# Decoder trunk on one core: ScalarE makes the high part of h, and the last norm's products are split over two engines

## What is computed

```
def rmsnorm(x, g):
    y = xf * lax.rsqrt(jnp.mean(xf * xf, axis=-1, keepdims=True) + EPS)
    return (y * g)
def swiglu(h, w_gu, w_down):
    gate, up = jnp.split(h @ w_gu, 2, axis=-1)
    return (jax.nn.silu(gate) * up) @ w_down
def layer(...):
    x = x + 0.5 * swiglu(rmsnorm(x, n1), ffn1_gu, ffn1_down)
    h = rmsnorm(x, n_mix)            # then h @ w_in, gated linear attention, window attention
    x = x + concatenate([o_g, o_s]) @ w_out
    x = x + 0.5 * swiglu(rmsnorm(x, n2), ffn2_gu, ffn2_down)
# after both layers: y = rmsnorm(x, norm_final)
```

## Time and profile before

| | us |
|---|---|
| runs of the kernel | 2183.99, 2188.75, 2182.62 |
| median | 2183.99 |
| profiled execution, span from first to last instruction | 2178.1 |
| TensorE busy in the span | 2116.3 (97%) |
| VectorE, ScalarE, GpSimd busy | 811.9, 581.5, 800.7 |

### The profile page before, as it was taken

How to read it: one execution, slowest core, us unless ns; L and a number is a source line. 1 busy time by engine, 2 the same in 40 slices (tenths; PEclk the granted TensorE clock), 3 DMA queues, 4 the chain that set the end, 5 groups by cost and what they waited for, 6 DMA issues and landing times.

```text
span 2178.1 us, 40378 instructions
## 1 busy us (share of the span) xinstructions
PE 2116.3 (97%) x16718; PEld 2078.8 (95%) x16718; DVE 811.9 (37%) x1125; ACT 581.5 (27%) x795; POOL 800.7 (37%) x337
## 2 busy tenths in 40 slices
PE   6999999999999999999999999999999999999996
PEld 6999999998889999999999999999898999999996
DVE  5222222486257222222332222226754452222224
ACT  3222222235233222222232222222532322222222
POOL 3333344432113333344433333444221233444443
PEclk9999999999889999999999999999997999999998
DMA  4222222421212222222222222233221122222222
GB/s 137 90 87 87 87 87 97 132 78 50 81 51 78 87 88 88 88 93 97 89 87 87 87 88 88 96 96 123 69 90 39 61 88 87 87 87 87 92 92 99
DMA packets 56869, 190.53 MB, mean 87 GB/s; under 512 B 8976, under 2 KB 10672, under 8 KB 56240
## 3 DMA queue, kind: packets, MB, share of 16 engines
q1 hardware_dynamic: 48960, 176.31, 25.0%
q10 hardware_dynamic: 7824, 13.00, 1.8%
HBM read 184.37 MB, written 6.95 MB: 88 GB/s over the span
## 4 chain that ended last, share of the span: by engine, by line
PE 92%; DVE 6%; issue 1%; ACT 0%; DMA 0%; DVEq 0%; ACTq 0%
PE ps L379 84%; DVE h_hi L989 2%; PE ps L538 1%; DVE ssum L1003 1%; PE ps L651 1%; PE ps L527 1%; DVE h_lo L992 1%; PE ps L444 1%; PE ps L645 1%; PE ps L690 1%; PE ps L718 0%; PE ps L510 0%; DVE x L1323 0%; PE ps L679 0%; PE ps L704 0%
## 5 line engine op out<-in xcount | busy, mean ns | idle before, releaser
L366 POOL TENSOR_TENSOR w_lo<-w_raw,w_hi 128x1024 fp32r<-128x1024 f32 x332 | 800.3, 2411 | 1359.4 <-ACT w_hi L745 1345.2
L379 PE MATMUL ps<-h_hi,w_hi 128*128 128x272 f32 x3424 | 718.8, 291 | 23.8 <-DVE h_lo L992 22.1
L379 PE MATMUL ps<-h_lo,w_hi 128*128 128x272 f32 x3424 | 712.9, 290 | 0.0
L379 PE MATMUL ps<-h_hi,w_lo 128*128 128x272 f32 x3424 | 710.8, 289 | 0.0
L745 ACT ACTIVATE w_hi<-w_raw 128x1024 fp32r<-128x1024 f32 x328 | 347.5, 1060 | 1349.2 <-PE ps L379 1349.1
L379 PEld LDWEIGHTS ps<-h_hi,w_hi 128*128 128x128 f32 x3424 | 544.1, 190 | 28.8 <-issue 24.8
L379 PEld LDWEIGHTS ps<-h_hi,w_lo 128*128 128x128 f32 x3424 | 543.4, 190 | 0.0
L379 PEld LDWEIGHTS ps<-h_lo,w_hi 128*128 128x128 f32 x3424 | 538.9, 190 | 0.0
L379 PE MATMUL ps<-act_lo,w_hi 128*128 128x272 f32 x1408 | 291.6, 289 | 0.0
L379 PE MATMUL ps<-act_hi,w_hi 128*128 128x272 f32 x1408 | 291.2, 288 | 0.0
L379 PE MATMUL ps<-act_hi,w_lo 128*128 128x272 f32 x1408 | 290.4, 288 | 0.0
(11 more groups left out here) (213 smaller groups left out, 1246.8 us busy)
## 6 DMA issues: line engine op xcount, KB each, us to landing
w_raw<-stream SPq DMA_DIRECT2D x332, 512.0 KB, 3.4
x<-xT ACTq DMA_DIRECT2D x8, 272.0 KB, 6.3
y_d<-x SPq DMA_DIRECT2D x8, 272.0 KB, 2.1
s<-s_d ACTq DMA_DIRECT2D x2, 1024.0 KB, 4.9
s_s_d<-s ACTq DMA_DIRECT2D x2, 1024.0 KB, 4.6
kc<-kc_d ACTq DMA_DIRECT2D x2, 512.0 KB, 5.2
vc<-vc_d ACTq DMA_DIRECT2D x2, 512.0 KB, 6.6
k_s_d<-kc_d ACTq DMA_DIRECT2D x2, 496.0 KB, 8.9
```

Of the source, the lines that this page charges most:

```text
L366: pool.tensor_tensor(w_lo[:, q, :], w_raw[:, q % RAW, :], w_hi[:, q, :].bitcast(F32), ALU.subtract).then_inc(lo_ready, 1)
L379: ins = pe.matmul(dst[:, hf, :], w[:, slot, cols], r[:, hf * TH:(hf + 1) * TH], start=first and w is w_hi and r is rhs_hi, stop=last and r ...
```

## The change

1. **ScalarE makes `h_hi`** (new `high_h`), as an activation Copy with the gain as scale, ahead of the Square of the same part; VectorE's `new_h` waits for it (`h_high`) and makes only `h_lo` and the addition. The additions get a semaphore of their own, `sq_added`. In the start ScalarE waits for the addition of part n−2 before it makes `h_hi` of part n (before, only its Square waited, for `h_step`). ScalarE now also waits for the load of the layer's parameters `lp` right after it has issued it.
2. **TensorE's first tile** waits for h part by part from part 0 on. In the first feed-forward of a layer it starts with the first part; before the second it still waits for five. Four waits on `down_used` are added ahead of the first four tiles.
3. **The last norm.** ScalarE multiplies x by the gain, seven parts ahead of the root and the eighth behind it, and copies the reciprocal `rs` to PSUM. VectorE multiplies parts 0, 2, 3, 5, 6 with the copy in PSUM, GpSimd parts 1, 4, 7 with `rs` in SBUF. SyncE still stores the parts in order, each with its own semaphore.

```diff
 def model_tile(dst, chunk, slot, hb=None):
...
-                    if hb is not None and k >= 5:
+                    if hb is not None:
                         pe.wait_ge(h_ready, hb + (k + 1))
...
-                pe.wait_ge(h_ready, hb + 5)
+                pe.wait_ge(h_ready, hb + (5 if half else 1))
                 for q in range(4):
+                    if half == 0:
+                        pe.wait_ge(down_used, l * (2 * KT) + (q + 1))
...
             def square(l, p, n):
                 act.wait_ge(x_ready, l * (3 * KT) + (p * KT + n + 1))
+                high_h(n, lp[:, LG + p * KT + n:LG + p * KT + n + 1])
                 dst = ssum[:, :] if n == 0 else sq_buf[:, n % 2, :]
                 act.activation(dst, x[:, n, :], ACT.Square).then_inc(sq_ready, 1)
+
+            def high_h(n, gain):
+                act.activation(h_hi[:, n, :], x[:, n, :], ACT.Copy, scale=gain).then_inc(h_high, 1)
...
                 if n >= 3:
-                    act.wait_ge(h_step, 2 * n - 2)
+                    act.wait_ge(sq_added, n - 2)
                 act.wait_ge(x_loaded[n], 16)
+                high_h(n, g_first[:, n:n + 1])
                 act.activation(dst, x[:, n, :], ACT.Square).then_inc(sq_ready, 1)
...
                 act.dma_start(lp[:, :], lparams[l]).then_inc(lp_loaded, 16)
+                act.wait_ge(lp_loaded, l * 16 + 32)
...
-            root(DEPTH * 3)
+            for n in range(KT):
+                act.wait_ge(h_ready, DEPTH * 3 * KT + n + 1)
+                if n == KT - 1:
+                    root(DEPTH * 3)
+                g = LG + 2 * KT + n
+                act.activation(x[:, n, :], x[:, n, :], ACT.Copy, scale=lp[:, g:g + 1]).then_inc(y_gained, 1)
+            act.wait_ge(rs_ready, DEPTH * 3 + 1)
+            act.activation(pair(2), halves(rs[:, :]), ACT.Copy).then_inc(rs_copied, 1)
...
-                dve.tensor_scalar(h_hi[:, n, :], x[:, n, :], gain, None, ALU.mult).then_inc(h_step, 1)
-                k = n + max(n - 2, 0) + 1
-                dve.wait_ge(h_step, step + k)
+                dve.wait_ge(h_high, squares + n + 1)
                 dve.scalar_tensor_tensor(out=h_lo[:, n, :], in0=x[:, n, :], scalar=gain,
                                          in1=h_hi[:, n, :].bitcast(F32), op0=ALU.mult,
                                          op1=ALU.subtract).then_inc(h_ready, 1)
...
+            pool.wait_ge(rs_ready, DEPTH * 3 + 1)
+            for n in Y_POOL:
+                pool.wait_ge(y_gained, n + 1)
+                pool.tensor_tensor(x[:, n, :], x[:, n, :], rs[:, :], ALU.mult).then_inc(y_ready[n], 1)
...
+            dve.wait_ge(rs_copied, 1)
             for n in range(KT):
-                dve.scalar_tensor_tensor(out=x[:, n, :], in0=x[:, n, :], scalar=lp[:, g:g + 1],
-                                         in1=rs[:, :], op0=ALU.mult, op1=ALU.mult).then_inc(y_ready, 1)
+                if n not in Y_POOL:
+                    dve.wait_ge(y_gained, n + 1)
+                    dve.tensor_tensor(halves(x[:, n, :]), pair(2), halves(x[:, n, :]),
+                                      ALU.mult).then_inc(y_ready[n], 1)
```

More of the change, by code:

```diff
@@ L303, in trunk @@
         h_ready = sem("h_ready")
-        h_step = sem("h_step")
+        h_high = sem("h_high")
+        sq_added = sem("sq_added")
+        y_gained = sem("y_gained")
+        rs_copied = sem("rs_copied")
         ssum_ready = sem("ssum_ready")
@@ L313, in trunk @@
         eps_set = sem("eps_set")
-        y_ready = sem("y_ready")
+        y_ready = [sem(f"y_ready{n}") for n in range(KT)]
         y_stored = sem("y_stored")
@@ L337, in earlier @@
             return sum(x[0] == step for x in STEPS[:pos])
-        B_STEPS = 2 * KT - 2
+        SQ_ADDS = KT - 2
+        Y_POOL = (1, 4, 7)
         N_LOADS = 9
@@ L352, in _ @@
             for n in range(KT):
-                sp.wait_ge(y_ready, n + 1)
+                sp.wait_ge(y_ready[n], 1)
                 sp.dma_start(y_d[:, n, :], x[:, n, :]).then_inc(y_stored, 16)
@@ L963, in _ @@
                 dst = ssum[:, :] if n == 0 else sq_buf[:, n % 2, :]
+                if n == 0:
+                    act.wait_ge(lp_loaded, 16)
                 if n >= 3:
-                    act.wait_ge(h_step, 2 * n - 2)
+                    act.wait_ge(sq_added, n - 2)
                 act.wait_ge(x_loaded[n], 16)
+                high_h(n, g_first[:, n:n + 1])
                 act.activation(dst, x[:, n, :], ACT.Square).then_inc(sq_ready, 1)
@@ L983, in rope_swap, with new_h @@
                 return [8 + i if i < 8 else i - 8 if i < 16 else i for i in range(32)]
-            def new_h(n, gain, step, squares):
-                dve.tensor_scalar(h_hi[:, n, :], x[:, n, :], gain, None, ALU.mult).then_inc(h_step, 1)
-                k = n + max(n - 2, 0) + 1
-                dve.wait_ge(h_step, step + k)
+            def new_h(n, gain, adds, squares):
+                dve.wait_ge(h_high, squares + n + 1)
                 dve.scalar_tensor_tensor(out=h_lo[:, n, :], in0=x[:, n, :], scalar=gain,
@@ L995, in new_h @@
                 if n >= 2:
-                    add_square(n - 1, squares + n, h_step)
+                    if n >= 3:
+                        dve.wait_ge(sq_added, adds + (n - 2))
+                    add_square(n - 1, squares + n, sq_added)
                 if n == KT - 1:
-                    dve.wait_ge(h_step, step + (k + 1))
+                    dve.wait_ge(sq_added, adds + (n - 1))
                     add_square(n, squares + KT, ssum_ready)
@@ L1016, in boundary @@
                         dve.wait_ge(lp_loaded, l * 16 + 32)
-                    new_h(n, lp[:, LG + p * KT + n:LG + p * KT + n + 1], l * (3 * B_STEPS) + (p + 1) * B_STEPS,
+                    new_h(n, lp[:, LG + p * KT + n:LG + p * KT + n + 1], l * (3 * SQ_ADDS) + (p + 1) * SQ_ADDS,
                           l * (3 * KT) + (p + 1) * KT)
@@ L1333, in _ @@
             dve.memset(eps[:, :], EPS).then_inc(eps_set, 1)
-            dve.wait_ge(lp_loaded, 16)
             for n in range(KT):
-                dve.wait_ge(x_loaded[n], 16)
                 new_h(n, g_first[:, n:n + 1], 0, 0)
@@ L1341, in _ @@
                 ffn_half(l, 1)
-            scale_ready(DEPTH * 3)
-            dve.wait_ge(rs_ready, DEPTH * 3 + 1)
+            dve.wait_ge(norm_root, DEPTH * 3 + 1)
+            dve.reciprocal(rs[:, :], rs[:, :]).then_inc(rs_ready, 1)
+            dve.wait_ge(rs_copied, 1)
             for n in range(KT):
-                g = LG + 2 * KT + n
-                dve.scalar_tensor_tensor(out=x[:, n, :], in0=x[:, n, :], scalar=lp[:, g:g + 1],
-                                         in1=rs[:, :], op0=ALU.mult, op1=ALU.mult).then_inc(y_ready, 1)
+                if n not in Y_POOL:
+                    dve.wait_ge(y_gained, n + 1)
+                    dve.tensor_tensor(halves(x[:, n, :]), pair(2), halves(x[:, n, :]),
+                                      ALU.mult).then_inc(y_ready[n], 1)
 def constants():
```

## The result

| | before | changed |
|---|---|---|
| median of 20 runs each, us | 2182.78 | 2186.59 |
| lowest and highest | 2179.86, 2188.75 | 2182.25, 2189.93 |
| ratio of the times | | 1.0015, 95% interval 1.0008 to 1.0022 |
| span of the profiled execution, us | 2178.1 | 2184.0 |

The changed kernel is 0.15% slower, some 3 us, inside the 0.3% that was called no change, and inside the forecast range. The profiled execution of the changed kernel took 2185.84 us, 1.84 more than its span.

The account below looks back on a forecast made before the run. TensorE was taken as the bound, busy 2116.3 of 2178.1 us, so only its waits could shrink. Boundaries −0.9 and −1.4, start +2.6, end +0.1 made +0.4 on the 2183.99 median: 2184.4 us, range 2179.0 to 2188.0.

Parts of the forecast that it names:

- the 0.3% that was called no change: Whole kernel: the smallest difference a measurement can tell from no change, 6.6 us; chance of staying within it 0.94.
- Boundaries: Between half layers: sums come sooner, gaining 0.43 us after feed-forward and 0.7 after mixer, each twice: −0.9 and −1.4.
- Start: First norm: new order of parts and TensorE's clock together make the product with `ones` later, +2.6 us.
- the order: Start: additions, ScalarE's copy and `h_lo` stand one behind the other; last addition at 30.6 instead of 29.1, +1.5 us.
- Clock: Start: broken-up first tile leaves the product with `ones` and tile 1's first matmuls at the low level, +1.1 us.
- ScalarE's copy: Making `h_hi` on ScalarE: 0.66 us for one part, taken from a copy of the same size and types.
- Rival (d): ScalarE's copy with a scale per partition is dearer, deciding from about 1.0 us; at twice 0.66, 2198 us; chance 0.03.
- No price at `lp` and weights: Between layers: ScalarE's 2.5 us wait for `lp` and its moved weight copies make nothing late; cost 0, at most 2.5.
- Stores: The end: full DMA engines limit the stores, 5.6 us from the first part on, so shorter products do not shorten them.
- the end: Last norm: first part of y 0.2 us later, less 0.1 for the last products; +0.1 us, bounds −1.9 and +0.7.
- ScalarE's seven multiplications by the gain: Last norm: 3.8 us from 2159.7 plus 1.3 of table load, ending at 2164.8, just ahead of the root at 2165.0.
- The sum: Whole kernel: boundaries −0.9 and −1.4, start +2.6 and end +0.1 make +0.4 us.

Follow-up runs that it names:

- five_parts: The changed kernel, but TensorE waits for five parts of h before its first tile, as before the change; 2184.14 us against 2182.32 before (ratio 1.0007).
- half_stores: The changed kernel, storing only the left half of the columns of each part of y; 2183.78 us in one run.
- root_first: The changed kernel with the last root ahead of ScalarE's wait for the last part of h, one gain earlier; 2187.04 us, ratio 1.0016 to the kernel before.
- root_mid: The changed kernel with the last root behind the fourth of ScalarE's eight gains; 2183.00 us in one run.
- between_only: The kernel before, with only ScalarE's `h_hi` between the half layers taken from the change; 2181.65 us against 2182.32 (ratio 0.9993).
- end_only: The kernel before with only the new end (gains, copy of `rs`, products, stores); 2183.31 us against 2182.56 (ratio 1.0000).
- start_vector: The changed kernel, but at the start VectorE makes `h_hi` again; 2183.34 us against 2182.32 before the change (ratio 0.9997).
- start_free: The changed kernel, but at the start ScalarE's `h_hi` waits for x alone and only its Square for the addition; 2185.31 us in one run.
- late_low: start_free's waits, the end of before; second weight copy just before part 7 of h, third and fourth behind it; 2180.7 us against 2184.44 before (ratio 0.9978).
- late_vector: late_low with VectorE making `h_hi` at the start; 2179.30 us against 2182.56 for the kernel before (ratio 0.9977).

## Why the prediction was right, and where it was off

**Right.** The forecast of no measurable change, for the reason given: what the boundaries win, the start loses.

- *Boundaries.* −0.43 and −0.7 were forecast, twice each. Measured in the changed kernel −0.59 and −0.68 (offsets +4.51 to +3.92, and +5.53 to +4.85), in the second layer the same (−0.59, −0.68). The mechanism is that of the earlier trace rows: `h_lo` ends 0.6 us after GpSimd. The first lies beyond the bound, the 0.43 us of idle time of the earlier trace rows. That reading was wrong by 0.16. Before and then changed, the last pair of the tile and the product:

```profile
426.80 0.41 PE L379 MATMUL ps<-h_lo,w_hi 128*128 128x272 f32 x2
```

```profile
431.31 0.41 PE L387 MATMUL ps<-h_lo,w_hi 128*128 128x272 f32 x2
431.56 1.16 PE L454 MATMUL ps<-ssum,ones 128*128 128x272 f32 x4
```

  Where TensorE waits for nothing, the next instruction starts 0.25 us after a pair that is written down with 0.41. Idle time is counted from the end of the 0.41, so a wait costs 0.16 more than it shows: from pair to product 0.84 us before (426.80 to 427.64) and 0.25 now, which is the 0.59.
- *Start.* +1.5 for the order; the column b − a gives +1.65. Clock +1.1; the four profiles with this start give 0.7, 0.8, 1.4 and 2.1 in c − b, mean 1.3. Together 2.9 against 2.6. The changed kernel's own profile has 4.5, of which 0.7 is a late start of ScalarE and 0.8 a clock worse than its mean: one profile was an unlucky draw, and only its repetition under other names showed that.
- *Why 1.65 and not 1.5.* The order itself costs what was forecast: the last addition ends 23.07 us after the first weight copy begins (29.88 + 1.48 − 8.29), where it was 21.54 (27.62 + 1.48 − 7.56), +1.53. The other 0.12 are clock: before, the product begins 0.06 us behind the last addition, now 0.18, since TensorE is still at its last pairs at the low rate (0.66 each). In five_parts, where it is not, b − a is 23.09.
- *ScalarE's copy.* With the gain it takes 0.75 us (mean 752 ns over 48), not the 0.66 of the earlier trace rows. Rival (d), a copy of 1.0 us or more, falls. In the changed kernel the Square, which has no such scale, takes 0.64 us and the copy with it 0.75. The Trainium skill (ScalarE: Activation LUTs, What ACT_TABLE_LOAD costs) adds about 93 ns for an operand that is read from a [128, 1] column, which is what the gain is; the trace agrees, 0.75 against 0.64, and the forecast had overlooked it. In the start's sum this is not seen; at the end it is.
- *No price at `lp` and weights.* TensorE has no wait for `w_lo`. ScalarE's wait for `lp` is 2.36 us at the start and 5.63 us between the layers, over twice the forecast's 2.5; both are covered: the product with `ones` behind the second is at 1101.15 where it was at 1096.32, an offset of +4.8 as ahead of it.
- *Stores.* From the first issue to the end 7.32 us where it was 7.37, at 402 GB/s. half_stores shows that this is the queue.

**Off: the end, +0.1 forecast, +1.3 measured.** The step that failed is "ScalarE's seven multiplications by the gain (7 × 0.54 = 3.8 from 2159.7, then 1.3 of table load) end at 2164.8, just ahead of the root at 2165.0". It was wrong twice. 0.54 was the spacing of instructions without a gain; these have 0.65, 4.57 in all. And the table load does not follow the gains: it waits for TensorE's product (idle 0.76). The eighth part of h was ready long before, at 2165.85 (2163.88 + 1.97), so it is the root's own wait that holds the load, though only where another wait stands right ahead of it (last section). root_first and root_mid give 0.76 and 0.60 us for moving it, together the 1.35 by which the root is late. The warning was in the working: 2164.8 against 2165.0 is a cover of 0.2 us, and what it costs if that cover is gone was not priced. (4.57 us of gains instead of 3.8 are 0.8 more, and less the cover of 0.2 that is the 0.60.) The bounds, −1.9 and +0.7, did not hold the value. The rest of the end is as forecast: copy 0.63, first product 0.75.

**The sum.** With the mean start (+2.9), boundaries (−2.5) and end (+1.3) the change costs 1.7 us, where +0.4 was forecast and the ratio says 1.7 to 4.8 us; this sum is at the interval's lower edge, and what the rest would be is not shown. The profiled span grew by 5.9: the start of that run takes 4.5 of it, boundaries and end −1.3, and some 2.7 lie in the mixers, which differ by as much between other runs (last section). That the forecast was right owes something to its width: the range was 9 us, and the end's error of 1.2 us is small in it.

## What to carry to other kernels

An instruction moved to an idle engine still has a place in a chain: follow who waits for it in turn, part by part, before counting it as hidden; here one wait put ahead of a copy instead of behind it cost 2.2 us. When two engines hold each other up over shared operands, look first at whether the other one's work is needed yet, since moving three weight copies gave more than moving the work. And where two things end within 0.2 us of each other in a forecast, price both orders.

## What the runs showed of the hardware

- **A table load can be held by the wait of its activation.** Where the root's wait for the product stands alone ahead of the root, the load runs before that wait ends: at 2159.15 before, where the product ends at 2165.55, at 2163.05 in between_only, at once behind the gains in root_first, and over 1.3 us before the root can start in root_mid. Where the wait for the eighth part stands right ahead of the root's, the load starts only with the product done, though the eighth part had long been there: 0.76 us after the gains in the changed kernel, 0.77 in half_stores, 1.94 in end_only. Why two waits in a row do this was not tried. The activation behind it begins at the load's end (2169.64 + 1.28, 2170.93).
- **The clock in the mixers differs from run to run.** Runs of one kernel differ by 8 us and more. The distance from the product with `ones` at 427 us to that at 696 is 268.8 us before, 267.7 in start_vector, 273.5 in five_parts, though their mixers are nearly the same code. In the second layer of before and of the changed kernel the granted clock is 1.00 from 1500 to 1620 and from 1720 to 1780 us. Between them it is lower and differs from run to run; the windows of before, and then of start_vector (columns as in the start's windows):

```profile
1660.00:1680.00 20.00, 18.98 (x137) 0.83 0.09 27
1680.00:1700.00 20.00, 19.02 (x137) 0.83 0.09 27
1700.00:1720.00 20.00, 20.00 (x153) 0.91 0.23 86
```

```profile
1660.00:1680.00 20.00, 19.37 (x129) 0.74 0.09 27
1680.00:1700.00 20.00, 19.02 (x124) 0.72 0.09 27
1700.00:1720.00 20.00, 20.00 (x121) 0.68 0.22 86
```

TensorE is busy about as long in both, with 53 fewer matmuls done in 60 us in the second. What decides it was not tried, nor whether it is the whole of the spread: each kernel has one profile.
- **A broken-up tile can cost clock.** Pieces of 1.1 to 1.7 us with gaps of up to 2.2 end with the granted clock at 0.50, and the next tile begins there: 0.7 to 2.1 us in four runs with the same code up to there, 0.2 in start_vector, 0.5 in start_free, 1.6 and 2.0 in late_low and late_vector, none in five_parts.
- **The clock column isn't the rate just behind a pause.** In the kernel before, TensorE's first pairs, from 20.72 us, take 0.66 us and start 0.45 apart, and those from 23.89 take 0.42 and start 0.25 apart; the column says 1.00 throughout.
